# Alternating the two projection banks between iterations of a gated delta kernel

## What is computed

```
proj = h @ w_in                       # q, k, v, z columns
qkv  = silu(causal_depthwise_conv(qkv, conv_w))       # 4 taps
q, k = l2norm(q), l2norm(k)           # 16 q/k heads of 128, 32 v heads
o    = gated_delta_rule(q, k, v, g, beta)             # chunked, triangular solve
o    = rmsnorm(o) * norm_w * silu(z)
y    = o @ w_out
```

## Time and profile before

| what | us |
|---|---|
| median of 3 runs | 2849.15 |
| lowest and highest | 2848.85, 2851.08 |
| the profiled execution's own time | 2848.96 |
| its span | 2847.0 |
| PE, DVE, ACT, POOL busy in the span | 2720.7, 1949.3, 1208.2, 812.5 |

### The profile page before, as it was taken

One profiled execution on the slowest core, in us unless ns is written; L12 is line 12 of the kernel. 1 busy time (PEld: TensorE's weight loads), 2 busy tenths in 40 slices (PEclk: granted clock), 3 DMA queues, 4 the chain that ended last, 5 costly groups with the idle time before them and its releaser, 6 DMA issues.

```text
span 2847.0 us, 51314 instructions
## 1 busy us (share of the span) xinstructions
PE 2720.7 (96%) x20214; PEld 2404.2 (84%) x20214; DVE 1949.3 (68%) x2285; ACT 1208.2 (42%) x1521; POOL 812.5 (29%) x554
## 2 busy tenths in 40 slices
PE   6999999999997999999999999969999999999998
PEld 4788988898895777888888888769899999999996
DVE  1377877787778677666666666676999898555554
ACT  2255455545544444333333333344333334433343
POOL 1066666666667510000000000001555552000000
PEclk8999999999999999999999999989999999999999
DMA  9866666676665666666665555535554555555554
GB/s 364 311 195 214 223 216 200 205 247 199 200 223 169 212 184 207 187 191 189 188 188 187 189 189 186 167 115 169 156 171 148 157 169 172 179 185 183 184 201 147
DMA packets 283920, 552.72 MB, mean 194 GB/s; under 512 B 16817, under 2 KB 54258, under 8 KB 282610
## 3 DMA queue, kind: packets, MB, share of 16 engines
q1 hardware_dynamic: 263632, 474.02, 52.7%
q0 software_dynamic: 19408, 76.06, 7.2%
q10 hardware_dynamic: 722, 0.28, 0.0%
HBM read 548.19 MB, written 2.10 MB: 193 GB/s over the span
## 4 chain that ended last, share of the span: by engine, by line
PE 79%; DVE 11%; ACT 4%; issue 2%; DMA 2%; POOL 1%; DVEq 0%; SPq 0%; ACTq 0%; POOLq 0%; PEld 0%
PE pg L1130 20%; PE pg L1117 14%; PE pg L821 13%; PE pd L1130 11%; PE pd L1117 7%; PE pg L812 4%; DVE wl L2059 2%; PE pd L736 2%; DMA arena<-in_mod_w 1%; DVE arena L2340 1%; PE pd L985 1%; DVE arena L2342 1%; PE pd L1003 1%; DVE arena L2335 1%; PE pg L842 1%
## 5 line engine op out<-in xcount | busy, mean ns | idle before, releaser
L2059 DVE TENSOR_TENSOR wl<-wr,wh 128x1024 fp32r<-128x1024 f32 x616 | 773.0, 1264 | 515.7 <-ACT wh L1582 512.5
L1582 ACT ACTIVATE wh<-wr 128x1024 fp32r<-128x1024 f32 x616 | 652.6, 1060 | 1004.8 <-PE pg L1117 344.6
L595 POOL TENSOR_TENSOR wl<-wr,wh 128x1024 fp32r<-128x1024 f32 x195 | 479.8, 2462 | 394.3 <-ACT wh L1391 394.1
L1117 PE MATMUL pg<-hh,wh 128*128 128x256 f32 x1536 | 438.4, 285 | 3.9 <-ACT arena L1700 2.5
L1117 PE MATMUL pg<-hl,wh 128*128 128x256 f32 x1536 | 434.6, 283 | 0.0
L1117 PE MATMUL pg<-hh,wl 128*128 128x256 f32 x1536 | 434.3, 283 | 0.0
L1391 ACT ACTIVATE wh<-wr 128x1024 fp32r<-128x1024 f32 x216 | 227.7, 1057 | 349.3 <-PE pg L821 219.9
L821 PE MATMUL pg<-hh,wh 128*128 128x256 f32 x1024 | 301.2, 294 | 14.8 <-ACT arena L1439 12.0
L1117 PEld LDWEIGHTS pg<-hh,wh 128*128 128x128 f32 x1536 | 294.4, 192 | 16.6 <-issue 13.6
L1820 DVE SCALAR_TENSOR_TENSOR arena<-arena,condt 128x512 f32<-128x512 f32 x240 | 282.4, 1177 | 32.4 <-DMA arena<-in_mod_w 26.9
L1117 PEld LDWEIGHTS pg<-hl,wh 128*128 128x128 f32 x1536 | 294.5, 192 | 0.0
(11 more groups left out here) (392 smaller groups left out, 5323.6 us busy)
## 6 DMA issues: line engine op xcount, KB each, us to landing
wr<-in_w_in SPq DMA_DIRECT2D x224, 512.0 KB, 3.9
wr<-in_ffn_w_gu SPq DMA_DIRECT2D x176, 512.0 KB, 4.4
wr<-in_gdn_w_in SPq DMA_DIRECT2D x128, 512.0 KB, 4.3
arena<-in_mod_w POOLq DMA_DIRECT2D x64, 1024.0 KB, 7.7
wr<-in_ffn_w_down SPq DMA_DIRECT2D x88, 512.0 KB, 3.6
arena<-in_mod_w SPq DMA_DIRECT2D x32, 1024.0 KB, 12.2
wr<-in_gdn_w_in SPq DMA_DIRECT2D x128, 256.0 KB, 2.9
wr<-in_gdn_w_out SPq DMA_DIRECT2D x56, 512.0 KB, 4.6
```

What stands on the lines that cost most here:

```text
L595: nc.gpsimd.tensor_tensor(wl[c % RING][:], wraw[c % 4], wh[c % RING][:].bitcast(F32), ALU.subtract)\
L1117: m = nc.tensor.matmul(bank[:, n * T:(n + 1) * T], w[s][:, k, n * P:(n + 1) * P], act[x][:, k0 + k, :], skip_group_check=True, start=(firs ...
L1582: a(wh[c % 4][:], wraw[c % 4], ACT.Copy).then_inc(s_hc, 1)
L2059: v.tensor_tensor(wl[c % 4][:], wraw[c % 4], wh[c % 4][:].bitcast(F32), ALU.subtract).then_inc(s_lc, 1)
```

## The change

Which bank a group uses is now a function of the iteration: `first_bank(g)` is 0 for iterations 0 and 1, then 1, 0, 1, 0, 1, 0. Groups q/k, v, z of iteration g take banks first, other, first. So z of iteration g-1 and q/k of iteration g never share a bank. The waits follow the banks: chunk 0 waits for `conv` of the iteration before's v, and chunk 8 for `z_out` of the iteration before. ACT and DVE must know the bank when the program is built, so their loops now run three trips with two iterations in the body.

```
+def first_bank(g):
+    return 0 if g == 0 else (g + 1) % 2
...
+        def group_bank(g, grp):
+            return pg[(first_bank(g) + grp) % 2]
...
-                if c == 0 and not first_g:
+                if c == 0 and g == 1:
+                    pe.wait_ge(s_zo, 1)
+                    pe.wait_ge(s_cd, 1)
+                elif c == 0 and not first_g:
+                    pe.wait_ge(s_cd, g * 2)
+                if c == 8 and g == 1:
+                    pe.wait_ge(s_cd, 2)
+                elif c == 8 and not first_g:
                     pe.wait_ge(s_zo, g)
-                    pe.wait_ge(s_cd, g * 2 - 1)
-                if c == 8 and not first_g:
-                    pe.wait_ge(s_cd, g * 2)
...
-                bank, first, last = pg[grp % 2], kp == 0, kp == 7
-                if first_g and grp == 2:
-                    bank = pd[1]
+                bank, first, last = pd[1] if first_g and grp == 2 else group_bank(g, grp), kp == 0, kp == 7
...
-            with act.Fori(0, NIT - 2) as j:
-                beside(j)
-                turn(j)
-            beside(NIT - 2)
-            turn(NIT - 2, lambda: (o_high(0), o_high(1)))
-            beside(NIT - 1, False)
+            with act.Fori(0, (NIT - 2) // 2) as i:
+                for odd in range(2):
+                    beside(i * 2 + odd, odd)
+                    turn(i * 2 + odd, odd)
+            beside(NIT - 2, 0)
+            turn(NIT - 2, 0, lambda: (o_high(0), o_high(1)))
+            beside(NIT - 1, 1, False)
...
-            with dve.Fori(0, NIT - 2) as j:
-                iteration(j)
-                finish(j)
-            iteration(NIT - 2)
+            with dve.Fori(0, (NIT - 2) // 2) as i:
+                for odd in range(2):
+                    iteration(i * 2 + odd, odd)
+                    finish(i * 2 + odd)
+            iteration(NIT - 2, 0)
```

More of the change, by code:

```diff
@@ L1425, in gate_tokens, with tap @@
                 a(tk[:, 6, :], pd[0][:, 512 + 4 * NH:512 + 5 * NH], ACT.Exp).then_inc(s_a0, 1)
[L1427 removed]
+            def tap(g, grp, bank):
                 if isinstance(g, int) and g == 0:
@@ L1433, in tap, with z_out @@
                 for n in range(4):
-                    a(pend[:, grp * 4 + n, :], pg[grp][:, n * T:(n + 1) * T], ACT.Copy,
+                    a(pend[:, grp * 4 + n, :], bank[:, n * T:(n + 1) * T], ACT.Copy,
                       scale=cwc[:, 3, grp * 4 + n:grp * 4 + n + 1]).then_inc(s_cv, 1)
-            def z_out(g):
+            def z_out(g, bank):
                 act.wait_ge(s_pk, g * NCH + (NCH + RING))
-                a(zpend.rearrange("p a b -> p (a b)"), (pd[1] if isinstance(g, int) and g == 0 else pg[0])[:], ACT.Copy)\
-                    .then_inc(s_zo, 1)
+                a(zpend.rearrange("p a b -> p (a b)"), bank[:], ACT.Copy).then_inc(s_zo, 1)
             def silu_qk(g):
@@ L1536, in _ @@
             gh(0, 22)
-            tap(0, 0)
+            tap(0, 0, group_bank(0, 0))
             gh(0, 23)
-            tap(0, 1)
+            tap(0, 1, group_bank(0, 1))
             silu_qk(0)
@@ L1542, in _ @@
             gh(1, 1)
-            z_out(0)
+            z_out(0, pd[1])
             gh(1, 2)
@@ L1547, in _, with beside @@
             gate_tokens()
-            def beside(j, taps=True):
+            def beside(j, odd, taps=True):
                 steps = delta(j, taps)
@@ L1562, in beside @@
                     if t == 8 and taps:
-                        tap(j + 1, 0)
+                        tap(j + 1, 0, group_bank(1 + odd, 0))
                     if t == 16 and taps:
-                        tap(j + 1, 1)
+                        tap(j + 1, 1, group_bank(1 + odd, 1))
                     if t in STEP_AT:
@@ L1569, in beside, with turn @@
                     pass
-            def turn(j, more=None):
-                z_out(j + 1)
+            def turn(j, odd, more=None):
+                z_out(j + 1, group_bank(1 + odd, 2))
                 if more:
@@ L1876, in _, with conv @@
             dve.wait_ge(s_cst, N_CST)
-            def conv(g, grp):
+            def conv(g, grp, bank):
                 for sh in range(1, 4):
@@ L1884, in conv @@
                         tile = grp * 4 + n
-                        m = stt(out=pend[:, tile, sh:T], in0=pg[grp][:, n * T:(n + 1) * T - sh],
+                        m = stt(out=pend[:, tile, sh:T], in0=bank[:, n * T:(n + 1) * T - sh],
                                 scalar=cwc[:, 3 - sh, tile:tile + 1], in1=pend[:, tile, sh:T],
@@ L1898, in squares @@
                 v.tensor_tensor(sqb, fq, fq, ALU.mult).then_inc(s_sq1, 1)
-            for _ in conv(0, 0):
+            for _ in conv(0, 0, group_bank(0, 0)):
                 pass
@@ L1914, in _ @@
             squares(0)
-            for _ in conv(0, 1):
+            for _ in conv(0, 1, group_bank(0, 1)):
                 pass
@@ L2030, in mods, with iteration @@
                     mod_half(base, t // 2, t % 2)
-            def iteration(j):
+            def iteration(j, odd):
                 steps = delta(j, True)
@@ L2037, in iteration @@
                     if t == 5:
-                        first = conv(j + 1, 0)
+                        first = conv(j + 1, 0, group_bank(1 + odd, 0))
                     if 5 <= t < 8:
@@ L2041, in iteration @@
                     if t == 13:
-                        second = conv(j + 1, 1)
+                        second = conv(j + 1, 1, group_bank(1 + odd, 1))
                     if 13 <= t < 16:
```

## The result

The changed kernel takes 2859.03 us (median of 6 runs, 2857.09 to 2864.73) against 2850.48 us for the kernel before, measured beside it (6 runs, 2848.85 to 2852.56). The ratio is 1.0037, with a 95% interval of 1.0028 to 1.0047: 0.37% slower, some 10 us. The forecast was 2851.0 with a range of 2835 to 2856; the time lies outside it, on the slow side. The profiled execution took 2859.01 us, its span is 2857.1 us.

A forecast was written before the change was run, and what follows sets the result against it. PE was taken to bound the delta phase, busy 96.84 of 98.85 us an iteration. 2848.96 + 6 x (2.16 - 2.16 + 0.34) gave 2851.0 us; range 2835 to 2856, the forecast's own 2848 to 2854 with chance 0.60.

The forecast's parts named there:

- The port takes it back: At each boundary DVE, held by POOL at their shared port, gives back the 2.16 us and loses 0.34 more.
- The hold of DVE: The last conv-tap copy is held through POOL's `low` of chunks 3 and 4, done at 376.35.
- The loop bodies and branches: Larger two-iteration bodies and their branches cost 0; at most 3.0 us at each of two seams, 6 us.
- The six waits: PE's waits for `z_out` at the boundaries into iterations 2 to 7 vanish: 2.16 us each, 13.0 us.
- POOL does not move: Behind the boundary POOL's `low` of chunks 2 and 3 and two DMA issues keep their times while PE comes 2.16 us earlier.
- So the last copy and L1933 come 0.43 and 0.30 us ahead of a `low`: DVE's last conv-tap copy and product of norms start just before `low` of chunk 3, so the copy is held.
- that pair is at its worst already, two holds in two: DVE's two modulation-weight products before the first solve step, 5.19 us under POOL's subtractions, were not expected to be held longer.
- Slower by a late second round: Rival: one more subtraction holds DVE's modulation products; PE's first solve step waits 1.5 us, 11 us in all: 2860, chance 0.12.
- The gain stays: Rival: DVE gets its last copy and product of norms through, 13.0 us gained: 2836.0, chance 0.25.
- one of L1845, L1846 or L1933 at 2.5 to 5.5 us: Sign: the second or third conv-tap copy or the product of norms takes that long behind POOL's two DMA issues.
- Iterations of 98.9 to 99.2: Sign: iterations of the changed kernel last 98.9 to 99.2 us, with PE still busy 96.8.
- a wait of the first solve step: Sign of being wrong: PE waits at the solve's first step, behind the boundary; the forecast gave no size with this sign.

The follow-up runs named there:

- 3_7_8b: pool_waits_3_7 with a third POOL wait, ahead of `low` of chunk 8, for DVE's first masked product of the solve (tc): 2852.00 us, ratio 1.0017 to the kernel before.
- 3_7_8: pool_waits_3_7 with a third POOL wait, ahead of `low` of chunk 8, for the later DVE result x2: 2887.60 us, ratio 1.0140 to the kernel before.
- pool_waits_4: The changed kernel with POOL waiting for DVE's product of norms (L1944) ahead of `low` of chunk 4: 2838.22 us, ratio 0.9966 to the kernel before.
- pool_waits_3_7: pool_waits_3 with a second POOL wait, for DVE's masked products, ahead of `low` of chunk 7: 2839.72 us, ratio 0.9970 to the kernel before.
- pool_waits_3: The changed kernel with POOL waiting for DVE's product of norms (L1944) ahead of `low` of chunk 3: 2840.30 us, ratio 0.9967 to the kernel before.
- mod_early: The changed kernel with POOL's two DMA issues of modulation weights moved ahead of `low` of chunk 2: 2842.76 us, ratio 0.9978 to the kernel before.

## Why the prediction was wrong

**Right.** The wait for z goes at all six boundaries. The port takes it back: DVE is held, and L945 waits for L1944. ACT's `z_out` and POOL's two issues start when they did (0.96 and 6.82 us behind the last z matmul, before 0.95 and 6.80). The hold of DVE ends where it was forecast, 13.15 us behind the last z matmul against 376.35 - 363.16 = 13.19. The loop bodies and branches cost nothing that shows. The last iteration's L945 starts where it did. The six waits are worth about 13 us once DVE is free of POOL (12.1 measured).

**The first step that failed** stands behind "POOL does not move": "So the last copy and L1933 come 0.43 and 0.30 us ahead of a `low`". It takes for granted that the first copy, at 370.44, still passes. I had taken a lead of over a microsecond, during the DMA issues, as enough. The runs show that it isn't: the first copy is the one held, with a lead of 1.21 us, as is the product of norms with 1.16. So behind the second subtraction stand two more copies and their semaphore steps, L1944 ends at 14.98 us, and the transposes start 0.75 us later than before and not 0.34. That is 6 x 0.41 = 2.5 us of the error. The row nearest to the assumption, which the earlier trace rows leaves out, spoke for it (DVE of the kernel before, at the first recurrence's start):

```profile
171.87 0.17 DVE L1844 COPY arena<-vc 128x8 f32 x1 [0.18 <-DVE arena L1927]
```

This copy has a lead of 0.85 us, also during the issues, and passes; it does so in the changed kernel too. It starts 0.74 us into the two issues, the held one 0.35 us. What lets the one through and not the other no run here separates.

**The second step that failed** is that the solve's first step got no term: "that pair is at its worst already, two holds in two". At full clock that step starts 1.42 us later than before, 0.67 more than the transposes, with a wait of 0.54: 6 x 0.67 = 4.0 us. It was another operation of DVE that was held by one subtraction more, the two masked products (4.34 us instead of 1.64), while the pair itself took 4.38 instead of 5.19.

**A third term was missing.** The falls of the granted clock, 3.9 us in this profile, had none, although a wait of 2.2 us in another place was forecast. Against these stand the 2.2 us less behind the last boundary, which did not repeat. 2.0 forecast + 2.5 + 4.0 + 3.9 - 2.2 = 10.2 us.

**The rivals.** "Slower by a late second round" has the right size (2860), and in part the right road: one more subtraction holds DVE ahead of the first solve step, and PE waits there. But it is held at another operation, the wait is 0.54 us and not 1.5, only the two boundaries at full clock have it, and the 8.5 us of six such iterations need the clock's 3.9 to come near its 11. That its size fits so well is luck. "The gain stays" is what the kernel does when POOL yields, at 2838 to 2840 rather than 2836. The range left out the slow rival with its 0.12, which held too little: the forecast's own range gave 0.5 us a boundary to what could be held besides.

**What would show it.** The forecast asked for one of L1845, L1846 or L1933 at 2.5 to 5.5 us; it was L1844, now L1855, at 5.99. The two subtractions without a gap were there. Iterations of 98.9 to 99.2 were 100.3 and more. Its own sign of being wrong, a wait of the first solve step, came as well.

## What to carry to other kernels

When a wait of the bound engine is removed, list what its followers meet in the time that they now come to, and not at the first meeting only: the second hold cost 0.67 us an iteration here, beside the first one's 0.75. Count an operation as held even when it starts a microsecond ahead of the other engine's run, if that run stands queued without a wait; one such copy passed here, at the first recurrence, and six did not. A single semaphore wait on the off-path engine, put where it has slack behind it, turned this change from 0.37% slower to 0.33% faster; one more such wait in a dense stretch cost 12 us (3_7_8b), and 48 us where it named a later result (3_7_8), against the version without it. The best kernels of the study, pool_waits_4 (2838.2), pool_waits_3_7 (2839.7) and pool_waits_3 (2840.3), beat both the kernel before and the changed one and can't be told apart.

## What the runs showed of the hardware

At six boundaries a DVE copy on SBUF that started while POOL issued DMAs was held through the POOL operations queued behind the issues, although these started 1.2 us later: 5.99 us with two subtractions, 3.66 with one, 0.43 with none queued. At the first recurrence one that started 0.85 us ahead of such a subtraction passed in 0.17 us. The Trainium skill, SBUF — State Buffer, section "Who interferes with whom", describes a lock on a port pair that DVE and GpSimd share, held for whole instructions and won by the first to issue. That the hold is counted in whole instructions, these runs show. That the first wins can't be read from the recorded starts: at the six boundaries the later start wins, in mod_early a copy that starts 0.10 us ahead of a subtraction gets through. Whether POOL asks for the lock before its recorded start, or DVE's recorded start is not yet its asking, no run here shows.

Between two subtractions with 0.28 us of gap one copy of 0.17 us got through (mod_early), between two without a gap none did at six boundaries. And shortly behind waits of PE of 2.0 to 2.6 us stretches of about 3.4 us at half clock came in some iterations and not in others, at places that differ from one execution to the next; what sets them stays open.
